# A mixer with compressed, selected and windowed attention rewritten inside a one-core transformer kernel: outputs by columns, gates as their own narrow block, probabilities weighted before they are turned

## The reference

```python
def nsa_attention(h, w_in, w_out, cmp_pe, cmp_w1, cmp_w2, pos):     # 16 heads, 4 groups, width 64
    q, kc, vc, ks, vs, kw, vw, g_logits = jnp.split(h @ w_in, splits, axis=-1)   # 2608 columns
    q = partial_rope(q, pos)
    kcmp = compress(partial_rope(kc, pos), cmp_pe[0], cmp_w1[0], cmp_w2[0])      # 15 compressed keys
    vcmp = compress(vc, cmp_pe[1], cmp_w1[1], cmp_w2[1])
    gates = jax.nn.sigmoid(g_logits)                                             # 3 for each head
    o_c = softmax(q kcmp * scale, masked) @ vcmp
    o_s = softmax(q ks * scale, causal) @ vs
    o_w = softmax(q kw * scale, causal) @ vw
    return (gates_0 * o_c + gates_1 * o_s + gates_2 * o_w) @ w_out

def compress(t, pe, w1, w2):      # windows of 32 tokens, every 16: 15 windows, 2048 numbers each
    return silu((windows(t) + pe) @ w1) @ w2
```

## Time and profile before

| | us |
|---|---|
| median of 3 runs | 2869.33 (2868.88 to 2869.65) |
| the profiled execution | 2868.55 |
| its span in the trace | 2866.8 |
| PE busy / DVE busy / ACT busy / POOL busy | 2800.5 / 1859.6 / 1545.4 / 149.5 |
| mixer `nsa`, from the first 280-column block to the second row group of the output projection | 102.0 |
| TensorE clock granted, mean | 0.995 |

### The profile page before, as it was taken

The page is one execution under the profiler, slowest core; times in us unless marked ns, Lnnn a source line. Parts: engine busy times, 40 slices in busy tenths (PEclk is TensorE's granted clock), DMA queues, the critical chain, the costliest instruction groups (busy, mean ns, idle before and its releaser), DMA issues.

```text
span 2866.8 us, 34870 instructions
## 1 busy us (share of the span) xinstructions
PE 2800.5 (98%) x13460; PEld 2296.2 (80%) x13460; DVE 1859.6 (65%) x2728; ACT 1545.4 (54%) x2656; POOL 149.5 (5%) x254
## 2 busy tenths in 40 slices
PE   8999999999999999999999999999999999999998
PEld 7887788888888888878888888788787788787786
DVE  6767776776567677646776766777654754645654
ACT  6547654655765465546655546665454444444442
POOL 1010100000000000000001001100100000000000
PEclk9999999999999999999999999999999999999999
DMA  8664466566456767642576675377664555653552
GB/s 262 225 227 165 155 213 244 190 227 215 160 169 209 247 189 242 210 142 74 191 241 217 214 255 186 111 230 247 213 209 147 195 188 191 217 198 127 191 189 88
DMA packets 358629, 559.41 MB, mean 195 GB/s; under 512 B 14624, under 2 KB 246048, under 8 KB 358208
## 3 DMA queue, kind: packets, MB, share of 16 engines
q1 hardware_dynamic: 350720, 535.02, 55.9%
q0 software_dynamic: 7600, 21.81, 2.2%
q10 hardware_dynamic: 144, 0.36, 0.0%
HBM read 556.03 MB, written 1.10 MB: 194 GB/s over the span
## 4 chain that ended last, share of the span: by engine, by line
PE 92%; DVE 5%; ACT 1%; issue 1%; POOL 1%; DMA 0%; SPq 0%; DVEq 0%; ACTq 0%; POOLq 0%
PE ps L664 39%; PE ps L729 26%; PE ps L670 19%; PE ps L634 4%; PE ps L840 1%; PE ps L809 1%; DVE LO L1528 1%; POOL ST L2079 0%; DVE XL L1569 0%; PE ps L817 0%; ACT SB L1344 0%; DVE M L1607 0%; DVE M L1646 0%; DVE E L1885 0%; DMA RAW<-in_ffn_w_in 0%
## 5 line engine op out<-in xcount | busy, mean ns | idle before, releaser
L664 PE MATMUL ps<-HI,XH 128*128 128x512 f32 (+1 forms) x2496 | 984.5, 395 | 5.4 <-DVE LO L1533 2.0
L664 PE MATMUL ps<-LO,XH 128*128 128x512 f32 (+1 forms) x2496 | 971.1, 389 | 0.0
L1528 DVE TENSOR_TENSOR LO<-RAW,HI 128x1024 fp32r<-128x1024 f32 x468 | 567.1, 1223 | 317.8 <-ACT HI L1186 314.9
L670 PE MATMUL ps<-HI,XL 128*128 128x512 f32 (+1 forms) x2496 | 769.6, 389 | 0.3
L1533 DVE SCALAR_TENSOR_TENSOR LO<-RAW,GC,HI 128x512 fp32r<-128x512 f32 (+1 forms) x896 | 622.3, 744 | 188.6 <-ACT HI L1193 186.0
L1186 ACT ACTIVATE HI<-RAW 128x1024 fp32r<-128x1024 f32 x468 | 490.1, 1059 | 447.7 <-PE ps L729 284.5
L1193 ACT ACTIVATE HI<-RAW,GC 128x512 fp32r<-128x512 f32 (+1 forms) x896 | 587.9, 714 | 157.5 <-PE ps L670 132.8
L664 PEld LDWEIGHTS ps<-HI,XH 128*128 128x128 f32 x2496 | 469.8, 188 | 102.8 <-DVE LO L1533 3.9
L670 PEld LDWEIGHTS ps<-HI,XL 128*128 128x128 f32 x2496 | 466.7, 188 | 105.8 <-DVE XL L1569 7.9
L664 PEld LDWEIGHTS ps<-LO,XH 128*128 128x128 f32 x2496 | 469.8, 188 | 92.3
L729 PE MATMUL ps<-HI,AH 128*128 128x512 f32 x880 | 273.6, 392 | 0.0
(11 more groups left out here) (182 smaller groups left out, 1951.6 us busy)
## 6 DMA issues: line engine op xcount, KB each, us to landing
RAW<-in_ffn_w_in SPq DMA_DIRECT2D x350, 512.0 KB, 4.7
RAW<-in_ffn_w_out SPq DMA_DIRECT2D x88, 1024.0 KB, 4.9
RAW<-in_w_ada SPq DMA_DIRECT2D x48, 1024.0 KB, 5.1
RAW<-in_w_in SPq DMA_DIRECT2D x44, 1024.0 KB, 5.1
RAW<-in_w_ffn_in SPq DMA_DIRECT2D x88, 512.0 KB, 4.8
RAW<-in_diff_w_in SPq DMA_DIRECT2D x24, 1024.0 KB, 5.0
RAW<-in_w_ffn_out SPq DMA_DIRECT2D x22, 1024.0 KB, 4.9
RAW<-in_moba_w_in SPq DMA_DIRECT2D x12, 1024.0 KB, 5.1
```

The costliest lines, as they stand in the source:

```text
L664: e.matmul(ps[:, b + t, 0:nw], XH[:, k, t * P:(t + 1) * P], q[s][:, c * nw:(c + 1) * nw], start=(k == 0 and q is HI), stop=False)
L670: i = e.matmul(ps[:, b + t, 0:nw], XL[:, k, t * P:(t + 1) * P], HI[s][:, c * nw:(c + 1) * nw], start=False, stop=(k == 7))
L1528: e.tensor_tensor(LO[n % NSPLIT][:, 0:w], RAW[t.buf][:, at[1] * w:(at[1] + 1) * w], HI[n % NSPLIT][:, 0:w].bitcast(F32), ALU.subtract).the ...
```

## The change

**Order of the projection.** The blocks of `nsa` are now (1024, 512), (1536, 512), (2048, 512), (0, 512), a block of 48 gate columns, and (512, 512): keys and values first, queries last. The gates are projected transposed (48 rows by 256 tokens: 24 matmuls of 256 columns), copied, transposed back and scaled. The windows of the compression are multiplied in two halves, after the third block and after the fourth; their weights no longer pass through `RAW` but are loaded into QT and TM, which are free then, the second half when the first has been used. The scores of unit 0, the gates' transposes and the small compression matmuls stand between the quarters of the last block. The sigmoid is now an exponential, an addition and a reciprocal.

**The loop.** A unit is now a pair of heads with selected (even u) or windowed keys (odd u), so both units of a pair follow each other and add up in one PSUM bank. The probabilities are multiplied with gate over sum before they are transposed: a quarter of each unit's two heads by DVE, three operations by POOL. ACT copies the first head's transposed probabilities, DVE the second head's. In `outputs_by_columns` the values are the stationary operand (64 columns, the two heads in the two halves of the array) and the probabilities move, so that the outputs come out transposed, 64 rows for each head; the compressed part is added to the same bank, and ACT and DVE copy a finished pair straight into XH and XL. The eight compressed scores are made the same way, 32 rows each, and transposed once. `clock()`, `in_place`, `outputs_flipped` and their buffers are gone from `nsa`. Three weight halves of the output projection are split inside the loop.

**For diff and moba too.** The maxima are written negative by the reduction (`negate=True`), the small multiplication behind it is gone; the factor 0.125 is applied where the turned queries are copied.

```diff
+NSA_BLOCKS = ((1024, 512), (1536, 512), (2048, 512), (0, 512), (2560, 48), (512, 512))
...
+            def windows_of(st, h):
+                if h == 0:
+                    e.wait_ge(s_used, steps[st.k - 1].w1)
+                else:
+                    e.wait_ge(s_wd, 2)
+                w = a["nsa_cmp_w1"]
+                e.dma_start(st.t["QT"][:, :, :], w[st.j, 0, h * 1024:(h + 1) * 1024, :].rearrange("(c p) n -> p c n", p=P)
+                            ).then_inc(s_cw, 16)
...
+                if t.kind == "w" and t.step.kind == "nsa" and t.n0 - t.step.w0 in (12, 22):
+                    windows_of(t.step, (t.n0 - t.step.w0) // 20)
...
+            def outputs_by_columns(st, u, b, first, v):
+                PT = st.t["PT"]
+                for kt in range(2):
+                    for j in range(2):
+                        o = e.matmul(ps[64 * j:64 * j + 64, b, kt * P:S], v(kt),
+                                     PT[:, u % 2, j, 0:S] if kt == 0 else PT[:, u % 2, j, S:S + P],
+                                     start=(first and kt == 0), stop=False, skip_group_check=True)
+                o.then_inc(s_mix, 1)
...
+                later_block(st, 2, 512)
+                doubled(2, 0)
+                e.wait_ge(s_e, 8)
+                windows(0)
+                later_block(st, 3, 512, lambda k2: doubled(3, 1) if k2 == 2 else None)
+                windows(1)
+                gates()
+                later_block(st, 5, 512, in_queries, 2)
+
+                e.wait_ge(s_kk, 2)
+                e.wait_ge(s_hc, 3)
+                compressed_scores(0)
+                e.wait_ge(s_cp, c["cp"] + 5)
+                unit_scores(1)
+                e.wait_ge(s_ex, c["ex"] + 1)
+                unit_scores(2)
+                queries_turned(5)
                 e.wait_ge(s_tn, c["tn"] + 12)
...
-                clock()
...
+                compressed_scores(1)
+
+                e.wait_ge(s_cr, 1)
+                turn(ps[:, 6, :], [x["CT"][:, half * S + t * P:half * S + (t + 1) * P] for t in range(2) for half in range(2)]
+                     ).then_inc(s_cs2, 1)
...
+                for u in range(17):
+                    if 1 <= u < 14:
+                        e.wait_ge(s_ex, c["ex"] + u + 1)
+                        unit_scores(u + 2)
+                    if u >= 1:
+                        turned(u - 1)
+                    if u >= 2:
+                        mixed(u - 2)
+                    if u in (2, 3):
+                        compressed_turned(u - 2)
...
             def maxima(st, i, b=None):
...
-                e.tensor_reduce(MX[:, i, 0, :], Y[:, :, 0:128], AX.X, ALU.max)
-                e.tensor_reduce(MX[:, i, 1, :], Y[:, :, 128:384], AX.X, ALU.max).then_inc(s_mx, 1)
-                e.wait_ge(s_mx, c["mx"] + i + 1)
-                e.tensor_scalar(NM[:, i], MX[:, i], -SCALE, None, ALU.mult).then_inc(s_nm, 1)
+                e.tensor_reduce(NM[:, i, 0, :], Y[:, :, 0:128], AX.X, ALU.max, negate=True)
+                e.tensor_reduce(NM[:, i, 1, :], Y[:, :, 128:384], AX.X, ALU.max, negate=True).then_inc(s_nm, 1)
...
+                SB, CG = st.t["SB"], st.t["CG"]
+                for u in range(16):
+
+                    e.wait_ge(s_cg, st.c["cg"] + u + 1)
+                    for j, t, c0, c1 in ((0, 1, 128, 384), (1, 0, 0, 128), (1, 1, 128, 384)):
+                        v = SB[:, u % 3, j, c0:c1]
+                        o = e.tensor_scalar(v, v, CG[:, u, t, j:j + 1], None, ALU.mult)
+                    o.then_inc(s_df, 1)
```

More of the change, by code:

```diff
@@ L1023, in tp_of @@
[L1023 to L1036 removed]
+                                i.then_inc(s_wd, 1)
@@ new lines, in gates @@
+                def gates():
+                    e.wait_ge(s_tn, c["tn"] + 8)
+                    for k2 in range(4):
+                        w = st.w0 + 16 + k2
+                        s = taken(w)
+                        for m in range(2):
+                            for v in (HI, LO):
+                                e.matmul(ps[:, 4, 0:S], v[s][:, m * 48:m * 48 + P], XH[:, 2 * k2 + m, :],
+                                         start=(k2 + m == 0 and v is HI), stop=False)
+                        for m in range(2):
+                            i = e.matmul(ps[:, 4, 0:S], HI[s][:, m * 48:m * 48 + P], XL[:, 2 * k2 + m, :],
+                                         start=False, stop=(k2 + m == 4))
+                        i.then_inc(s_used, 1)
@@ new lines, in gates_turned, with compressed_scores @@
+                def gates_turned():
+                    e.wait_ge(s_gq, 1)
+                    for t in range(2):
+                        i = e.transpose(ps[:, 4, S + 48 * t:S + 48 * t + 48], x["GT"][:, t * P:(t + 1) * P], ident[0:48, 0:48])
+                    i.then_inc(s_gf, 1)
+                def compressed_scores(half):
+                    for p in range(4 * half, 4 * half + 4):
+                        r0 = 32 * (p % 4)
+                        i = e.matmul(ps[r0:r0 + 32, 6, half * S:half * S + S], KC[:, p // 2].rearrange("p u n -> p (u n)"),
+                                     QT[:, p, :], start=True, stop=True)
+                    i.then_inc(s_cq, 1)
@@ new lines, in turned @@
+                def turned(u):
+                    SB = x["SB"]
+                    e.wait_ge(s_df, c["df"] + u + 1)
+                    e.wait_ge(s_d0, c["d0"] + u + 1)
+                    if u >= 1:
+                        e.wait_ge(s_pt, c["pt"] + u)
+                        e.wait_ge(s_p1, c["p1"] + u)
+                    for j in range(2):
+                        o = turn(ps[:, (2 if u == 15 else 4) + j, :], [SB[:, u % 3, j, m * P:(m + 1) * P] for m in range(3)])
+                    o.then_inc(s_pf, 1)
@@ L1058, in nsa, with compressed @@
-                mixed(15)
+                    elif u % 2 == 0 and p >= 2:
+                        e.wait_ge(s_ol, c["ol"] + p - 1)
+                    outputs_by_columns(st, u, 6 + p % 2, u % 2 == 0, value(u))
+                    if u == 2:
+                        compressed(0)
+                    elif u % 2 == 1 and p >= 1:
+                        compressed(p)
+                def compressed(p):
+                    if p == 0:
+                        e.wait_ge(s_vb, 4)
+                    for j in range(2):
+                        o = e.matmul(ps[64 * j:64 * j + 64, 6 + p % 2, 0:S], VB[:, p // 2, (2 * p + j) % 4, :],
+                                     PTC[:, p // 2:8:4, :], start=False, stop=True, skip_group_check=True)
+                    o.then_inc(s_co, 1)
@@ new lines, in pair_high @@
+                def pair_high(p):
+                    e.wait_ge(s_co, c["co"] + p + 1)
+                    e.activation(XH[:, p, :], ps[:, 6 + p % 2, 0:S], ACT.Copy).then_inc(s_oh, 1)
+                first_head(0)
+                e.wait_ge(s_cm, 3)
+                e.activation(PC[:, :, :, 0:15], PC[:, :, :, 0:15], ACT.Exp, scale=1.0).then_inc(s_ce, 1)
+                for u in range(3, 18):
+                    if u < 16:
+                        exps(st, u)
+                    first_head(u - 2)
+                    if u in (3, 4):
+                        t = u - 3
+                        e.wait_ge(s_ct, t + 1)
+                        e.activation(PTC[:, 4 * t:4 * t + 4, :], ps[:, 7, :].rearrange("p (c n) -> p c n", n=P), ACT.Copy
+                                     ).then_inc(s_cc, 1)
+                    if u % 2 == 1 and u >= 5:
+                        pair_high((u - 5) // 2)
+                    if u in (8, 10, 12):
+                        split(st.w0 + 24 + (u - 6) // 2)
@@ L1886, in nsa @@
+                split(st.w0 + 15)
+                rotated(2)
+                split(st.w0 + 22)
+                rotated(3)
+                split(st.w0 + 24)
+                e.wait_ge(s_gs, 1)
+                e.tensor_scalar(GS[:, :, :, :], GS[:, :, :, :], 1.0, None, ALU.add).then_inc(s_gs, 1)
+                e.wait_ge(s_gs, 2)
+                e.reciprocal(GS[:, :, :, :], GS[:, :, :, :]).then_inc(s_gs, 1)
                 e.wait_ge(s_hs, 2)
@@ L1888, in nsa @@
                 pc = PC[:, :, :, 0:15]
-                for i in range(2):
-                    maxima(st, i)
                 e.wait_ge(s_vc, 1)
@@ L1894, in nsa @@
                                     cst("bmask").unsqueeze(2).to_broadcast([P, 4, 64]), ALU.mult).then_inc(s_vb, 1)
+                maxima(st, 0)
+                weights(0)
+                rotated(4)
+                maxima(st, 1)
+                maxima(st, 2)
+                weights(1)
                 e.wait_ge(s_z, 3)
```

484 lines of the change are left out of this document (237 added, 247 removed).

## The result

| | before | after |
|---|---|---|
| median, us | 2869.65 | 2857.02 (2855.52 to 2857.52) |
| profiled execution, us | 2868.55 | 2856.40 |
| its span, us | 2866.8 | 2854.5 |

The ratio of the means is 0.9953, with a 95% interval of 0.9938 to 0.9968; the gain is 12.6 us by the medians and 12.15 by the two profiled executions, where the forecast had 14.9. The time lies 2.5 us above the forecast of 2854.5, inside its own range and the wide one.

What follows compares the result with a forecast made beforehand. PE was taken as the bound, busy 2800.5 of 2866.8 us. In nsa 16.0 + 7.2 + 11.9 + 46.8 + 5.5 + 1.0 = 88.4 against 102.0; with diff 14.9 less, 2854.5 us (own range 2850 to 2858, wide range to 2866).

Steps and rivals of the forecast that it cites:

- the 102.0 us: Stages of the nsa step before the change, from behind four full blocks to the output projection's second row group; forecast 88.4.
- Projection, windows and what stands between the quarters: In nsa ahead of the loop: projection 16.0 us where 16.5 stood, windows 7.2, their layout hidden beside a block.
- no transfer was late: Rival for nsa's windows: at half the transfer rate PE waits 4 to 5 us for the second 2 MB, 2859; chance 0.10.
- The gap: From nsa's projection to its loop: 11.9 us, of which PE waits 4.8 (bounds nothing and 8.8) behind a chain.
- The loop: nsa's 16 units: 46.8 us, with PE's work 40.4 and outputs 0.68 us a unit instead of 1.38.
- Drain: Rival in nsa's loop: each change into and out of the halves costs 0.27 us, 5 us showing, 2859.5; chance 0.12.
- The loop's waits: In nsa's loop: 6.4 us (bounds 3 and 12), from three splits and the compressed softmax holding up units.
- The clock: TensorE's clock around nsa's loop start: expected to fall once, costing 1 us (bounds 0 and 3.3).
- That it stays down: Rival: TensorE's clock does not return before nsa's output projection, costing 20 to 35 us, 2878; chance 0.04.
- POOL: Multiplications in nsa's loop: 1.6 to 2.4 us a unit, setting the pace from 2.6; rival at 3.8 gives 2868, chance 0.12.
- Behind the loop: First row group of nsa's output projection: 5.5 us instead of 6.37, and the 2.2 us wait for a split goes.
- diff: Maxima without the third DVE operation in two diff mixers: 1.3 us gained (bounds 0 and 2.5), moba nothing.

Runs made afterwards that it cites:

- full_array: Changed kernel with outputs and compressed parts of nsa's loop over the full array, the second head's part left out: 2855.47 us, ratio 0.9950.
- extra_inside: Changed kernel with three more small full-array matmuls per unit of nsa's loop, one behind each of the first three output matmuls: 2877.05 us, ratio 1.0028.
- early_splits: Changed kernel with the three splits of output weights moved from inside nsa's loop to ahead of it: 2854.14 us, ratio 0.9945.
- clock_kept: Changed kernel with four matmuls of 384 columns filling PE's waits between projection and loop of nsa: 2857.58 us, ratio 0.9954.
- old_maxima: Changed kernel with the old positive maxima and third DVE operation back in diff and moba alone: 2858.71 us, ratio 0.9959.

## Why the forecast came out as it did, step by step

The forecast of the 102.0 us was 88.4, and with the 26.95 us ahead of them 115.35. The trace has 119.30, 3.95 more.

- **Projection, windows and what stands between the quarters** (1216.05 to 1269.65): 52.85 forecast, with the turn of the last queries counted in the gap; 53.60 measured. The overlap of halves in the windows held, no transfer was late, DVE's windows' layout was hidden. 0.75 short over 54 us, in parts that I did not take apart.
- **The gap**: 9.2 forecast in the same count, 9.32 measured. Waits of 4.8 were forecast, 0.8 + 1.9 + 1.5 came, for the block's copy, the turned queries and the copied compressed scores, as named.
- **The loop** is the term that was sized wrong: 47.8 forecast with the clock's 1.0, 50.6 measured (49.34 and 1.23 for unit 15 in the row group). The mechanism was right, outputs went from 1.38 to 0.70 and 0.80, but PE's work was undersized. I priced each operation as it stands beside its like. Read from the rows of the pair, transposes ahead of outputs take 0.09 more, outputs 0.12 more ahead of scores and 0.02 ahead of the compressed part, that part 0.07: 16 x 0.09 + 8 x 0.12 + 8 x 0.02 + 8 x 0.07 = 3.1 us. `full_array` shows that 2.3 of them come with the halves; the rest is the way into the scores' half rows, which that run pays too. The rival "Drain" was thus a part of the truth that I set aside because the earlier trace rows show only 0.06 on another change. By the Trainium skill, TensorEngine Tiling (Array Packing), Key Properties, a change of tiling mode drains TensorE: the runs agree that a change costs time, 0.25 us for a way in and out (`extra_inside`). That is not the 0.54 of the rival, and its 5 us were too many: without the halves the loop's main part is 1.3 us shorter, since waits fill up what is freed.
- **The loop's waits**: 6.4 forecast, 4.2 measured as idle time, about 5.0 by the starts. The splits were forecast at 3 x 1.1 and cost 3 x 0.92, which `early_splits` gave back; the compressed softmax cost 1.1 of idle time and not 3.
- **The clock**: forecast to fall once and cost 1.0; it fell once, and `clock_kept` prices it at 0.4. That it stays down did not happen in any run, `full_array` with some 7 us at the low level included.
- **POOL**: 1.6 to 2.4 us a unit forecast, 2.5 measured, hidden. The threshold of 2.6 was not tested: 2.5 is hidden, 3.28 sets the pace. The earlier trace rows had given the right bounds, 0.92 us for 256 columns.
- **Behind the loop**: no wait for a split, as forecast; 5.5 forecast for the first row group, 5.81 measured (7.04 less 1.23).
- **diff**: 1.3 forecast, 1.75 measured and shown by `old_maxima`. With 0.1 in the rest of the output projection and 0.7 behind 1857.32, where the kernels are the same, this accounts for the gap between 14.9 and 12.15: 3.95 less 0.45, less 0.8. The 0.7 is luck, by the clock's falls in the two executions, so the changed parts gave about 11.5 of the 14.9, and the forecast came nearer than they did.

Read by the starts, the loop's 2.8 us are 3.1 of PE's work more (2.3 of them shown by `full_array`), 1.4 of waits less, 0.6 more for work at the low clock (1.6 where 1.0 was forecast, and `clock_kept` shows that most of it hides waits), and 0.5 that is left over. This 0.5, the 0.75 of the projection and 0.3 of the row group are differences between rows that no run took apart.

## What to carry to other kernels

Price an operation by the distance to what follows it in the new order, not beside its like: each change between the full array and its halves cost 0.10 to 0.15 us, and using the halves cost 0.145 us a unit, a fifth of the outputs that it made twice as fast. In a loop where PE is busy 35.6 us of 38.7 and DVE, ACT and POOL 28.8 to 29.4 each, work with slack (here the splits of later weights) belongs where they idle, ahead of the loop; that alone gave 2.8 us. A wait that is one of several in a chain moves instead of vanishing, so ask first which engine's list of operations ends last there.
